# An order of side work in two FFNs: one piece a step, modulation chunks behind eight steps of their own

## The reference

```python
def second_block(x, c, mod_w, mod_b, ...):
    for l in range(DEPTH):
        mod = (silu(c) @ mod_w[l] + mod_b[l]).reshape(bsz, N_SUB, 3, D_MODEL)
        x = post_add(x, swiglu(pre(x, 0), ffn_w_in[l, 0], ffn_w_out[l, 0]), 0, FFN_RES)
        y = token_mixer(pre(x, 1), ...)          # needs lam_bar, b_bar and c of s5_ssm
        x = post_add(x, y, 1, 1.0)
        x = post_add(x, swiglu(pre(x, 2), ffn_w_in[l, 1], ffn_w_out[l, 1]), 2, FFN_RES)

def swiglu(h, w_in, w_out):                      # h 256x1024, w_in 1024x5632, w_out 2816x1024
    gate, up = jnp.split(h @ w_in, 2, axis=-1)
    return (jax.nn.silu(gate) * up) @ w_out
```

## Time and profile before

| | us |
|---|---|
| median of 3 runs (2119.06 to 2129.02) | 2123.0 |
| profiled execution, its own time | 2125.95 |
| its span in the profile | 2124.2 |
| TensorE busy, of the span | 1950.9 (92%) |
| VectorE busy | 1540.6 (73%) |
| ScalarE busy | 984.4 (46%) |
| GpSimd busy | 245.0 (12%) |
| share of the 16 DMA engines | 48.1% |

### The profile page before, as it was taken

The page is one execution under the profiler, slowest core; times in us unless marked ns, Lnnn a source line. Parts: engine busy times, 40 slices in busy tenths (PEclk is TensorE's granted clock), DMA queues, the critical chain, the costliest instruction groups (busy, mean ns, idle before and its releaser), DMA issues.

```text
span 2124.2 us, 34037 instructions
## 1 busy us (share of the span) xinstructions
PE 1950.9 (92%) x14000; PEld 1813.8 (85%) x14000; DVE 1540.6 (73%) x2265; ACT 984.4 (46%) x1551; POOL 245.0 (12%) x190
## 2 busy tenths in 40 slices
PE   6897999987979998998889998999899989998998
PEld 6796899987958997988879888998898889888997
DVE  5866688878556897688667666898777667666555
ACT  5523444454235444545443455444546543445444
POOL 1020011110201111111100000111111100001111
PEclk9998999989989999999989999999999989999999
DMA  5320599523215984445523345896444523244552
GB/s 206 119 98 21 195 341 359 215 100 114 85 54 225 357 328 166 169 161 236 234 103 120 120 156 208 339 374 252 145 172 170 183 96 140 100 169 147 181 179 100
DMA packets 53291, 384.23 MB, mean 181 GB/s; under 512 B 5904, under 2 KB 6032, under 8 KB 6928
## 3 DMA queue, kind: packets, MB, share of 16 engines
q1 hardware_dynamic: 53136, 382.05, 48.1%
HBM read 380.98 MB, written 1.05 MB: 180 GB/s over the span
## 4 chain that ended last, share of the span: by engine, by line
PE 72%; DVE 16%; ACT 6%; issue 4%; DMA 1%; SPq 0%; DVEq 0%; ACTq 0%
PE stream L436 14%; PE stream L437 14%; PE stream L438 14%; PE works L450 5%; PE works L451 5%; PE works L452 5%; DVE w_lo L1030 3%; ACT w_hi L775 3%; DVE mx L1139 2%; DMA raw<-w 1%; PE stream L488 1%; DVE mx L1227 1%; PE works L612 1%; PE stream L489 1%; PE works L697 1%
## 5 line engine op out<-in xcount | busy, mean ns | idle before, releaser
L436 PE MATMUL stream<-h_hi,w_hi 128*128 128x256 f32 x2976 | 854.5, 287 | 23.5 <-DVE w_lo L1030 23.3
L437 PE MATMUL stream<-h_lo,w_hi 128*128 128x256 f32 x2976 | 847.9, 285 | 0.0
L438 PE MATMUL stream<-h_hi,w_lo 128*128 128x256 f32 x2976 | 847.6, 285 | 0.0
L1030 DVE TENSOR_TENSOR w_lo<-raw,w_hi 128x1024 fp32r<-128x1024 f32 x572 | 736.2, 1308 | 145.8 <-ACT w_hi L775 119.4
L775 ACT ACTIVATE w_hi<-raw 128x1024 fp32r<-128x1024 f32 x572 | 588.3, 1050 | 131.7 <-PE works L452 82.0
L436 PEld LDWEIGHTS stream<-h_hi,w_hi 128*128 128x128 f32 x2976 | 576.9, 194 | 32.8 <-issue 29.9
L437 PEld LDWEIGHTS stream<-h_lo,w_hi 128*128 128x128 f32 x2976 | 577.3, 194 | 2.6 <-issue 0.5
L438 PEld LDWEIGHTS stream<-h_hi,w_lo 128*128 128x128 f32 x2976 | 576.9, 194 | 0.0
L1506 POOL TENSOR_TENSOR g_lo<-hid,g_hi 128x256 fp32r<-128x256 f32 x140 | 191.9, 1372 | 1589.9 <-ACT g_hi L805 1589.9
L933 ACT ACTIVATE gate_t<-stream 128x256 f32<-128x256 f32 x132 | 50.6, 384 | 408.0 <-PE stream L438 405.2
L450 PE MATMUL works<-w_hi,g_hi 128*128 128x512 f32 x528 | 207.5, 393 | 4.2 <-DVE w_lo L1030 4.1
(11 more groups left out here) (368 smaller groups left out, 2271.1 us busy)
## 6 DMA issues: line engine op xcount, KB each, us to landing
raw<-w SPq DMA_DIRECT2D x294, 1024.0 KB, 4.8
mx<-w SPq DMA_DIRECT2D x64, 1024.0 KB, 7.0
par<-p_in SPq DMA_DIRECT2D x2, 1110.0 KB, 7.5
x<-x_in SPq DMA_DIRECT2D x1, 1024.0 KB, 6.7
mx<-bt_in SPq DMA_DIRECT2D x2, 512.0 KB, 5.6
out<-x SPq DMA_DIRECT2D x4, 256.0 KB, 2.4
con<-const_in SPq DMA_DIRECT2D x1, 968.0 KB, 4.7
par<-p_in SPq DMA_DIRECT2D x1, 225.0 KB, 6.8
```

What stands on the lines that cost most here:

```text
L436: mm(o, hi, r_hi[:, kt, :], start=first, stop=False, skip_group_check=True)
L437: mm(o, hi, r_lo[:, kt, :], start=False, stop=False, skip_group_check=True)
L438: last = mm(o, lo, r_hi[:, kt, :], start=False, stop=end, skip_group_check=True)
L1030: v.tensor_tensor(w_lo[:, q % SLOTS, :], raw[:, chunk_of_unit[q] % RAWS, (q % 2) * UNIT:(q % 2 + 1) * UNIT], w_hi[:, q % SLOTS, :].bitcast ...
```

## The change

In the first FFN of each second-block layer:

- three of the large coefficient pieces are cut in two, so that `coef` has steps 0 to 9 instead of 0 to 6. The instructions are the same and in the same order;
- `COEFS` is reordered to 20 entries, one ahead of each matrix step from the ninth to the 28th;
- in layer 0 the eight modulation chunks are not spread over the FFN (`behind_ffn`) but put by the new `behind_steps` behind matrix steps number 3, 4, 5, 6 and 28, 29, 30, 31 (counted from 0). That gives gu 2, down 0, `mod 4`, gu 3, `mod 5`, gu 4, `mod 6`, down 1, `mod 7`, gu 5 at the front and gu 19, `mod 8`, gu 20, `mod 9`, down 9, `mod 10`, gu 21, `mod 11`, down 10 at the end. Before they stood behind gu 6, gu 8, gu 10, gu 12, gu 14, gu 16, gu 18 and gu 19.

```diff
-COEFS = [("coef", 0), ("coef", 1), ("coef", 2), ("coef", 3), ("coef", 4), ("table", 0), ("table", 1), ("coef", 5),
-         ("coef", 6), ("table", 2), ("kzero", 0), ("table", 3), ("bzero", 0), ("table", 4), ("table", 5), ("table", 6),
-         ("table", 7)]
+COEFS = [("coef", 0), ("coef", 1), ("coef", 2), ("coef", 3), ("coef", 4), ("table", 0), ("coef", 5), ("table", 1),
+         ("coef", 6), ("coef", 7), ("kzero", 0), ("table", 2), ("coef", 8), ("table", 3), ("coef", 9), ("table", 4),
+         ("bzero", 0), ("table", 5), ("table", 6), ("table", 7)]
+RAW_MODS = {3: 0, 4: 1, 5: 2, 6: 3, 28: 4, 29: 5, 30: 6, 31: 7}
...
+def behind_steps(steps, which, mods, at):
+
+    ffn = [k for k, s in enumerate(steps) if s[2] in ("gu", "down")][which * FFN_STEPS:(which + 1) * FFN_STEPS]
+    out = []
+    for k, s in enumerate(steps):
+        out.append(s)
+        if k in ffn and ffn.index(k) in at:
+            out.append(mods[at[ffn.index(k)]])
+    return out
...
-        behind_ffn(behind_ffn(second_block(0), 0, MODS[1][4:12]), 1, MODS[1][12:]) + second_block(1)
+        behind_ffn(behind_steps(second_block(0), 0, MODS[1][4:12], RAW_MODS), 1, MODS[1][12:]) + second_block(1)
...
                         link(TTn(t1, cim, wide(t["kr"]), ALU.mult))
+                    elif i == 5:
                         TTn(cp[:, 0, 0], cp[:, 0, 0], t0, ALU.subtract)
                         STT(cp[:, 0, 1], cp[:, 0, 1], -1.0, t1, ALU.mult, ALU.subtract).then_inc(s_cre_done, 1)
                         dve.wait_ge(s_cre_done, L + 1)
-                    elif i == 5:
+                    elif i == 6:
...
                         link(TTn(t1, cp[:, 0, 0], wide(t["li"]), ALU.mult))
+                    elif i == 7:
                         TTn(cp[:, 1, 0], cp[:, 1, 0], t0, ALU.add)
                         link(TTn(cp[:, 1, 1], cp[:, 1, 1], t1, ALU.subtract))
-                    else:
+                    elif i == 8:
...
                         link(TTn(t1, bim, wide(t["lr"]), ALU.mult))
+                    else:
                         link(TTn(o0, o0, t0, ALU.subtract))
```

## The result

Over ten runs of each the changed kernel has a median of 2139.35 us (2136.66 to 2142.48), the kernel before one of 2129.65 us (2119.06 to 2133.53). The ratio is 1.005, 95% interval [1.0035, 1.0065]: slower by 7 to 14 us. The three runs of before that the prediction started from had a median of 2123.0. The medians are 9.7 us apart; the forecast was +12.9 us, which is inside the interval.

The account below looks back on a forecast made before the run. TensorE carries 72% of the chain, so a change counts where TensorE starves. Front +16.2, middle -17.5, end +17.2 and layer 1 -3.0 sum to +12.9 us on the median of 2123.0: 2136 us, range 2127 to 2146.

Parts of the forecast that it names:

- The rule: Layer 0's FFN: a chunk waits until two coming steps are lowered, so the four-buffer ring fills and loads become one serial chain.
- The links: Load, lowering and modulation per link of the serial chain: long 13.9 us (13.3 without a `g_hi`), short 10.6 us.
- (b): Same mechanism with shorter links, second loads landing 1.0 us sooner and no step at the lower clock: -5.5, 2130 us; 17%.
- (c): Loads issued together land together, the first taking 7.3 instead of 4.8 us: 2142 us; 8%.
- Front: Layer 0's FFN up to the start of `gu 7`: +16.2 us, bounds +14 and +19.
- Middle: Layer 0's FFN, `gu 7` to the end of `gu 19`, no chunks left: -17.5 us, bounds -19 and -14.5.
- End: Layer 0, last matmul of `gu 19` to the beginning of `post`: +17.2 us, bounds +14 and +20.
- Layer 1: Layer 1's FFN, new coefficient order and no chunk: its idle goes, -3.0 us, bounds -3.5 and +1.
- Sum: Whole kernel: +16.2 - 17.5 + 17.2 - 3.0 = +12.9 us, 2136 us on the median's level.
- slower: Whole kernel measured slower by more than the 0.5%, 10.6 us, that a measurement tells from no change; 72%.
- Rival (a): The change does what it says: chunks do not make the ring serial, -21.6 - 3.0, 2098 us; 5%.
- two causes: TensorE's waits for `w_lo` in the kernel before come from VectorE (chunk and large piece together 6.7 us) and the weight ring.

Follow-up runs that it names:

- Experiment 3: Changed kernel, with ScalarE and VectorE no longer preparing the next two steps' weights ahead of the eight chunks; 2112.03 us, ratio 0.9933 to the kernel before.
- experiment 7: Changed kernel with its places and lookahead, VectorE's chunk work on data already in SBUF, the eight loads left out; 2101.6 us, ratio 0.9886 to the kernel before.
- 8: Changed kernel, chunks used without lookahead and placed behind steps 1, 3, 5, 7, 9, 25, 28, 30; 2102.79 us, ratio 0.9882 to the kernel before.
- experiment 1: Kernel before with only the coefficient pieces halved and reordered, chunks spread as before; 2118.48 us, ratio 0.9968 to the kernel before.
- experiment 5: Kernel before with only the two-step lookahead ahead of its eight ring chunks taken away; 2121.1 us, ratio 0.9977 to the kernel before.
- experiment 6: Kernel before with pieces halved and reordered, chunks spread as before but used without lookahead; 2108.03 us, ratio 0.9919 to the kernel before.

## Why the prediction was right, step by step

- **The rule** (a chunk is used only after the next two steps are lowered, so chunks behind every step fill the ring): right. Experiment 3 takes it away and gets 29.8 us back in this FFN; experiment 7 keeps it and takes away the loads that it holds up, and gets 36.2. A ring of more than four buffers was not tried.
- **The links.** Long links were put at 13.9 and 13.3 us, short ones at 10.6. Measured between bursts: 14.2, 13.5 and 10.6 in front, 14.5, 13.0 and 10.6 (1075.81 to the end of the last chunk, 1086.4) at the end. Second loads landed 7.9, 7.2, 8.2 and 7.3 us after their burst (7.5 taken), first ones 4.8 and 4.9 (4.8 taken). The fit of the Trainium skill ("DMA: Bandwidth & Descriptors", section "Anatomy of one DMA") gives an estimate of 4.4 and 6.8 us for the two; the page gives it for loads issued from GpSimd, which the prediction did not say, and these are issued by SyncE. They lie above it, and the measured ones decide. Rivals (b) and (c) fall with these: the four seconds took 7.6 us on average, not 6.5, and firsts did not wait for seconds. In the eleven traces no load of the ring landed ahead of the one issued before it, in 1232 pairs that were in flight together.
- **Front**: +16.2 forecast, +16.8 measured. Within it the first chunk ended 0.9 us later than I put it, because the load of `gu 4` landed only by 879.2, 6.6 us after its issue at 872.6, where I had taken about 5 (the last section says what stood beside it). Waits of 4.5, 6.2 and 1.8 us ahead of `down 1`, `gu 5` and `gu 6` stand for the 3, 8 and 4 forecast: `down 1` and `gu 5` ran partly at the lower clock (7.1 and 7.4 us), which shortened the waits behind them and cost nothing more, as the loads set the pace.
- **Middle**: -17.5 forecast, -18.0 measured; no wait is left in it.
- **End**: +17.2 forecast, +17.3 measured. `post` was put at 44.8 us behind the end of `gu 19` and came 44.8 behind it. `gu 21` and `down 10` waited 6.2 and 5.9 us, for the 6 and 8 forecast; `gu 21` ran partly at the lower clock (7.5 us), which shortened the second wait.
- **Layer 1**: -3.0 forecast, -3.4 measured; the idle is gone.
- **Sum**: +12.9 forecast, +12.5 in the two FFNs, +11.1 between the profiled spans and +9.7 between the medians. The stretches agree to 0.6 us each, so the mechanism was right. The whole time of 2136 us against 2139.35 measured is another matter: it was set on a median of 2123.0 that further runs moved to 2129.65, and in the sessions of the experiments the same kernel had medians of 2125.98 to 2126.75. That the miss is only 3.4 us is partly luck: the base was 6.65 us too low and the difference of the medians 3.2 us smaller than forecast. By the prediction's own line of 10.6 us, the medians' 9.7 stay just short of the "slower" to which it gave 72%, though the interval leaves out no change.
- **Rival (a)**, the change doing what it says, is what experiments 3 and 8 come near to. It was not wrong about VectorE's room: experiment 7 shows that room to be enough for all eight chunks. It was wrong about the ring.

One statement at the head of the prediction fared worse, that two causes, VectorE's pieces and the ring, stand behind the waits of the kernel before. Each edit alone gained 1.1 us (experiment 1) and 6.1 (experiment 5) in layer 0's FFN, both together 11.8 (experiment 6), of 22.9 over the floor. The trace of before shows a third cause, which the prediction left out. Of TensorE's longer waits 3.57 and 3.10 us stand behind a chunk and a large piece and 2.88 behind a load, but 2.74 behind a chunk beside a `table` step, with ScalarE's rounding held up by the sine:

```profile
1016.07 1.06 ACT L957 ACTIVATE mx<-mx 128x1024 f32<-128x1024 f32 x1 [4.54 <-DVE mx L1399]
```

The sum did not depend on it, since the change took the chunks away from pieces and tables altogether.

## What to carry to other kernels

In a ring of buffers that one queue fills in order, ask of every new tenant how many later tenants must be in and used before it can leave: with four buffers, a chunk that waits for two more steps, and a chunk behind each step, that number is the ring, and prefetching turns into a chain of load, prepare, use (13 us a step here against 5.8). Side work that shares the ring should be used first and spaced second; the kernel that did both gained 1.2%, where moving the work alone lost 0.5%. And an edit that takes one cause away can put another in its place, as the new order of the pieces put tables beside chunks: read the waits that are left before saying what the first cause was worth.

## What the runs showed of the hardware

Two things I had not expected. In the changed kernel the load of `gu 4`, 1 MB with no other load of the ring beside it, landed after 6.6 us instead of 4.8. It was not the 0.5 MB of `bt` issued 0.4 us behind it: in the kernel before the load with `bt` behind it (858.5) landed after 4.7 us, and in layer 1 the same pair gave 4.7 to 4.9 us in all eleven traces. What stood beside it is a packet of 16 KB of the profile's queue of instructions (`q8 instruction` in the view of the DMA queues), started at 872.6. Over the eleven traces, loads of the ring that were alone in flight took 4.6 to 5.4 us where no such packet started during them, and 4.6 to 7.3 us where one did. So the packet goes with every landing later than 5.4 us, though not every packet delays a load; that it is the cause was not tested.

And TensorE's clock was lost in places by waits of some 3 us and kept in others. Inside these FFNs every step behind a wait of up to 2.26 us kept a granted clock of 1.00. Of the steps behind longer ones, from 2.50 us (experiment 1, 0.77) to 6.2, all but one fell to 0.64 to 0.79; the one kept 1.00 behind 2.78 us (experiment 3, `gu 21`, 5.9 us). A gate/up step then took 7.3 us in most cases instead of 5.8, and 8.5 and 8.3 behind 3.2 and 3.7 us in experiment 1, at 0.64 and 0.67; `down 1` behind 4.5 us in the changed kernel took 7.1 at 0.76. So the price of a wait is not the wait alone, it is 0 to 2.7 us more, and the length of the wait does not settle which.
